# The first gather of each expert stage reads its indices from where VectorE writes them, and VectorE's first low parts wait for it

## The reference, cut to what matters

```
def ec_moe(h, w_router, w_gate, w_up, w_down):
    cap = EC_CAPACITY * length // N_EXPERTS          # 128 of 1024 tokens, 32 of 256
    aff = jax.nn.softmax((h @ w_router).astype(jnp.float32), axis=-1)
    g, idx = lax.top_k(jnp.swapaxes(aff, 1, 2), cap)
    xg = jax.vmap(lambda hb, ib: hb[ib])(h, idx)
    hid = jax.nn.silu(jnp.einsum('becd,edf->becf', xg, w_gate)) * jnp.einsum('becd,edf->becf', xg, w_up)
    out = jnp.einsum('becf,efd->becd', hid, w_down) * g.astype(h.dtype)[..., None]
    return ...                                       # each row added back at its token
```

## Time and profile before

| | us |
|---|---|
| median of 3 runs | 2653.34 |
| the runs | 2649.62 to 2656.38 |
| the profiled execution | 2649.22 |
| its span | 2647.40 |
| TensorE busy | 2354.5 (89%) |
| VectorE busy | 1793.8 (68%) |
| ScalarE busy | 1417.3 (54%) |
| GpSimd busy | 191.8 (7%) |

### The profile page before, as it was taken

How to read it: one execution, slowest core, us unless ns; L and a number is a source line. 1 busy time by engine, 2 the same in 40 slices (tenths; PEclk the granted TensorE clock), 3 DMA queues, 4 the chain that set the end, 5 groups by cost and what they waited for, 6 DMA issues and landing times.

```text
span 2647.4 us, 33888 instructions
## 1 busy us (share of the span) xinstructions
PE 2354.5 (89%) x13012; PEld 1791.6 (68%) x13012; DVE 1793.8 (68%) x1983; ACT 1417.3 (54%) x1435; POOL 191.8 (7%) x222
## 2 busy tenths in 40 slices
PE   5999998789739999999999969998791999999994
PEld 3787777568626666666666647776571788888883
DVE  5623222465577888878888756566557899999995
ACT  6400112565515666666656543666351777777773
POOL 0000000000010101101101010000000011111110
PEclk9899999899859999999999979999895999999997
DMA  6024545545306877877878751010543899999995
GB/s 241 24 84 133 164 149 132 224 168 210 141 28 262 283 289 289 296 295 285 306 274 284 295 166 29 28 44 20 200 152 135 322 394 390 388 388 388 387 379 182
DMA packets 194244, 585.53 MB, mean 221 GB/s; under 512 B 19560, under 2 KB 64352, under 8 KB 187616
## 3 DMA queue, kind: packets, MB, share of 16 engines
q1 hardware_dynamic: 178592, 529.61, 53.8%
q0 software_dynamic: 12336, 48.24, 6.7%
q10 hardware_dynamic: 3216, 6.29, 0.6%
HBM read 536.88 MB, written 47.21 MB: 221 GB/s over the span
## 4 chain that ended last, share of the span: by engine, by line
PE 84%; DVE 7%; DMA 4%; ACT 4%; issue 1%; SPq 0%; POOL 0%; ACTq 0%; POOLq 0%; DVEq 0%
PE ps L1506 14%; PE ps L1508 14%; PE ps L1507 14%; PE ps L1519 6%; PE ps L544 5%; PE ps L545 4%; PE ps L546 4%; PE ps L767 3%; PE ps L769 2%; PE ps L768 2%; PE ps L486 1%; PE ps L520 1%; PE ps L1527 1%; PE ps L581 1%; PE ps L582 1%
## 5 line engine op out<-in xcount | busy, mean ns | idle before, releaser
L1715 DVE TENSOR_TENSOR R_H_r<-R_M,R_W_r 128x2048 fp32r<-128x2048 f32 x336 | 761.3, 2288 | 148.0 <-ACT R_W_r L1620 147.9
L1620 ACT CAST R_W_r<-R_M 128x2048 fp32r<-128x2048 f32 x336 | 640.5, 1914 | 220.9 <-PE ps L1508 86.7
L1508 PE MATMUL ps<-R_W_r,R_C_r 128*128 128x512 f32 x1536 | 609.3, 397 | 0.0
L1506 PE MATMUL ps<-R_W_r,bc_r 128*128 128x512 f32 x1024 | 415.0, 405 | 13.2 <-DVE R_C_r L1733 9.5
L1507 PE MATMUL ps<-R_H_r,bc_r 128*128 128x512 f32 x1024 | 405.6, 396 | 0.0
L1508 PEld LDWEIGHTS ps<-R_W_r,R_C_r 128*128 128x128 f32 x1536 | 291.1, 190 | 66.9
L544 PE MATMUL ps<-R_H_r,R_W_r 128*128 128x512 f32 (+1 forms) x632 | 233.3, 369 | 16.6 <-DVE R_W_r L885 8.9
L1506 PEld LDWEIGHTS ps<-R_W_r,bc_r 128*128 128x128 f32 x1024 | 194.2, 190 | 70.9 <-issue 17.4
L545 PE MATMUL ps<-R_C_r,R_W_r 128*128 128x512 f32 (+1 forms) x632 | 229.3, 363 | 0.0
L546 PE MATMUL ps<-R_H_r,R_W_r 128*128 128x512 f32 (+1 forms) x632 | 228.8, 362 | 0.0
L1507 PEld LDWEIGHTS ps<-R_H_r,bc_r 128*128 128x128 f32 x1024 | 194.5, 190 | 43.2
(11 more groups left out here) (290 smaller groups left out, 3696.3 us busy)
## 6 DMA issues: line engine op xcount, KB each, us to landing
R_M<-in_moe_w_gate SPq DMA_DIRECT2D x114, 1024.0 KB, 8.2
R_M<-in_moe_w_down SPq DMA_DIRECT2D x112, 1024.0 KB, 7.7
R_M<-in_moe_w_up SPq DMA_DIRECT2D x110, 1024.0 KB, 7.4
bc<-in_ada_w SPq DMA_DIRECT2D x28, 1024.0 KB, 4.9
R_H<-in_moe_w_up SPq DMA_DIRECT2D x18, 1024.0 KB, 9.5
R_H<-in_moe_w_down SPq DMA_DIRECT2D x16, 1024.0 KB, 10.4
R_H<-in_moe_w_gate SPq DMA_DIRECT2D x14, 1024.0 KB, 10.0
R_W<-in_ev_w_in SPq DMA_DIRECT2D x25, 512.0 KB, 4.0
```

The costliest lines, as they stand in the source:

```text
L1506: pe.matmul(o, hi[:, k, :], wh[:, kk, cs], start=(k == 0), stop=False)
L1508: ins = pe.matmul(o, lo[:, k, 0:P], wh[:, kk, cs], start=False, stop=(k == KC - 1))
L1620: nc.scalar.copy(whi[j], raw[slot + j]).then_inc(unit_high_done, 1)
L1715: nc.vector.tensor_tensor(wlo[j], raw[slot + j], whi[j], ALU.subtract).then_inc(unit_low_done, 1)
```

## The change

The last of the 16 ranking rounds overwrites nothing any more, and the wait that follows it is for the index search instead. GpSimd's first gather in each layer has a function of its own, `gather_first`: it reads its indices from column 0 of `icolT` (column 32 for the context) instead of from `gidx`, with no copy, and then raises `gather_index_set` (and `context_gather_index_set`), which the copies raised before. VectorE waits for that semaphore (the context's in layer 0) before its first two low parts. GpSimd's wait for `tokens_chosen` stands behind its waits for the stores, where it stood ahead of them. The other gathers are as before.

```
             for r in range(CAPL // 8):
                 v8, i8 = tkv[0:ne, 8 * r:8 * r + 8], tki[0:ne, 8 * r:8 * r + 8]
                 own.do(nc.vector.max(v8, a))
-                nc.vector.max_index(i8, v8, a)
-                own.do(nc.vector.match_replace(a, v8, a, -2.0))
+                ins = nc.vector.max_index(i8, v8, a)
+                if r < CAPL // 8 - 1:
+                    own.do(nc.vector.match_replace(a, v8, a, -2.0))
+            own.do(ins)
...
+            dve.wait_ge(context_gather_index_set if C else gather_index_set, n0 + 1)
             low(0, 0, 0, 0, 0)
             low(0, 0, 0, 0, 1)
             token_columns(n0, 0)
...
-            def gather(count, first):
+            def gather_first():
+
+                pool.indirect_dma_start(out=xg, out_offset=None, in_=xnd,
+                                        in_offset=bass.IndirectOffsetOnAxis(ap=icolT[:, 0:1], axis=0)).then_inc(rows_gathered, 16)
+                pool.sem_inc(gather_index_set, 1)
+                if C:
+                    pool.indirect_dma_start(out=xgc[0:C, :], out_offset=None, in_=xnd,
+                                            in_offset=bass.IndirectOffsetOnAxis(ap=icolT[0:C, 32:33], axis=0)).then_inc(context_rows_gathered, 16)
+                    pool.sem_inc(context_gather_index_set, 1)
+
+            def gather(count):
...
-            pool.wait_ge(tokens_chosen, l + 1)
-
             pool.wait_ge(normed_stored, 16 * (NT if l == 0 else NT + TL))
             for b in range(2):
                 pool.wait_ge(tile_stored[b], 16 * (NT // 2 if l == 0 else NT // 2 + TL // 2))
-            gather(n0 + 1, True)
-            gather(n0 + 2, False)
+            pool.wait_ge(tokens_chosen, l + 1)
+            gather_first()
+            gather(n0 + 2)
```

More of the change, by code:

```diff
@@ L1849, in pool_moe @@
             C = CAPC if l == 0 else 0
-            def gather(count, first):
+            def gather_first():
[7 more added lines that the diff above has]
+            def gather(count):
                 n, e = count - 1, count - 1 - n0
-                if not first:
-                    pool.wait_ge(rows_gathered, n * 16)
-                    pool.wait_ge(rows_transposed, n)
+                pool.wait_ge(rows_gathered, n * 16)
+                pool.wait_ge(rows_transposed, n)
                 pool.tensor_copy(gidx[:, 0:1], icolT[:, bass.ds(e, 1)]).then_inc(gather_index_set, 1)
                 if C:
-                    if not first:
-                        pool.wait_ge(context_rows_gathered, n * 16)
+                    pool.wait_ge(context_rows_gathered, n * 16)
                     pool.tensor_copy(gidx[0:C, 1:2], icolT[0:C, bass.ds(e + 32, 1)]).then_inc(context_gather_index_set, 1)
@@ L1898, in pool_moe @@
                 pool.wait_ge(tile_stored[b], 16 * (NT // 2 if l == 0 else NT // 2 + TL // 2))
-            gather(n0 + 1, True)
-            gather(n0 + 2, False)
-            gather(n0 + 3, False)
-            gather(n0 + 4, False)
+            pool.wait_ge(tokens_chosen, l + 1)
+            gather_first()
+            gather(n0 + 2)
+            gather(n0 + 3)
+            gather(n0 + 4)
             scatter(n0 + 1, True)
             with pool.Fori(n0 + 5, n0 + NE + 1) as count:
-                gather(count, False)
+                gather(count)
                 scatter(count - 3, False)
```

## The result

| | before | after |
|---|---|---|
| median of 7 runs, us | 2650.72 | 2638.35 |
| the runs, us | 2647.34 to 2656.38 | 2635.09 to 2643.72 |
| the profiled execution, us | 2649.22 | 2639.8 |
| its span, us | 2647.4 | 2638.1 |
| mean granted clock of TensorE | 0.941 | 0.944 |

What follows compares the result with a forecast made beforehand. The prediction took TensorE to bound the kernel, with uncovered waits before each expert stage setting its start. Layer 0's 4.78 us and layer 1's 6.49 gave 11.27 off 2653.34: 2642.1 us, forecast range 2638 to 2646.

Steps and rivals of the forecast that it cites:

- the loss of 0.33 us priced for layer 0: Layer 0's context gather, blocked by a low part, lands at about +6.6, delaying the token columns; bounds 0 and 2.3 us.
- (1): Ranking in both layers: without the last MATCH_REPLACE the cast follows the index search directly; gain 0.65 us twice, 1.30.
- (2): First gathers: index copies and their wait go, VectorE releases the gather directly; gain 4.46 us in layer 0, 2.25 in layer 1.
- (3): VectorE's new wait before its low parts: they start about +0.5 us after layer 0's gather start, 0.0 in layer 1.
- tie as going to the gather: Layer 1: gather and low part start together, the gather is not blocked; landing 4.28 against 7.87 us, gain 3.59.
- (A): Rival: VectorE's low part wins layer 1's tie and blocks the gather; total gain 8.0, 2645.3 us; chance 0.24.
- Layer 1's landing: Layer 1's gathered rows land in 4.28 us instead of 7.87, gain 3.59, weight load leaving behind the gather's descriptors.
- (4): After the starts: the second gather's copy, layer 0, may inherit any of the 4.38 us that isn't VectorE's doing.
- (B): Rival: GpSimd's first use costs about 2 us on layer 0's gather; total gain 7.1, 2646.2 us; chance 0.07.
- (C): Rival: VectorE is ahead in both layers, blocking GpSimd through both low parts; only 1.30 stays, 2652.0 us; chance 0.04.
- (D): Rival: the load stream, not TensorE, sets the second expert stage; layer 1 gains nothing, 2648.6 us; chance 0.05.
- (E): Rival: TensorE's half-clock stretches lengthen by 0.74 us each, outweighing the gain; with 18, 2655.4 us; chance 0.04.

Runs made afterwards that it cites:

- e1: Changed kernel with the last MATCH_REPLACE put back; median 2637.63 us, ratio 0.9950 to the kernel before.
- e8: Changed kernel with VectorE's first two low parts waiting, in both layers, for the landing of the first gathered rows; 2639.44 us, one run.
- e4: Changed kernel with layer 1's increment ahead of the gather, so that VectorE's low part starts first; 2637.12 us, one run.
- e3: Kernel before, index copies kept, without the last MATCH_REPLACE and with VectorE's low parts waiting for the copies; 2642.29 us, ratio 0.9975.
- e6: Changed kernel without VectorE's wait, plus a small GpSimd memset in layer 0 released by the end of the ranking; 2641.64 us, one run.
- e5: As e4, with SyncE's first weight load of layer 1 held until the gathered rows have landed; 2633.32 us, one run.
- e7: Changed kernel with the wait on the gather itself, gates computed behind the token choice, token-column semaphore raised earlier; 2635.89 us, ratio 0.9949 to before.
- e9: Changed kernel without VectorE's wait in layer 1; in layer 0 it waits only for its own last token-choice operation; 2640.54 us, one run.
- e2: Changed kernel without VectorE's wait for the increment, gathers still straight; 2645.89 us, ratio 0.9980 to the kernel before.

## Where the prediction was right, and where it was wrong

The direction held, and so did the mechanism but for one step; the sizes in the sum did not all hold. The forecast was 2642.1 and the time 2638.35, 3.75 us lower, inside the range of 2638 to 2646 but only 0.35 above its lower end. The step that failed is the loss of 0.33 us priced for layer 0, which did not come. The term of the sum that was mis-sized most is its base, 2653.34 where seven runs gave 2650.72. Both are worked out below, with the terms in the prediction's order.

(1) *The last replacement.* Priced at 0.65 twice; e1 gives 0.66 and 0.61. Right. The cast starts 0.04 behind the search's end where 0.03 was said.

(2) *The copies.* The gather was to start 0.82 behind VectorE's last operation of the token choice (the copy L1309) and starts 0.85 behind it (763.68 to 764.53). From the index search to the gather it is 5.08 and 2.89 us less; 5.11 and 2.90 were priced for parts (1) and (2).

(3) *The order.* "GpSimd's queue runs ahead of its cores": right. The increment came 0.22 us before the gather, VectorE 0.56 behind it in layer 0 (0.5 said) and 0.01 ahead of it in layer 1 (0.0 said). The "tie as going to the gather" did so three times in three. That it did is the part the forecast did not earn: the starts were worked out as equal, the gather was taken as the winner with no row that says so, and 3.3 of the 11.27 us hung on it; (A) had the other outcome at 0.24. "Only the DMA's first moment is open to it" held both ways: a gather already begun loses nothing (1.01), the context's, which met a running low part, ended 0.78 behind that part's end at 767.38 (+3.6, as said).

The Trainium skill's exclusive lock ("SBUF — State Buffer", "SBUF: two separate sides") agrees with the half in which VectorE comes first, from a lead of 0.08 us on; with the lead of 0.01 in layer 1 the gather was not blocked. Its other half would hold the low part until the gather ends; a low part begun at 765.09, 0.45 us before the gather's end, was not held, nor did the two take longer (4.49 us).

**The step that failed** is the loss priced for layer 0: "ends at +2.8 + 0.8 = +3.6 [...] thus 2.9 behind its descriptors, so at about +6.6 [...] Loss 0.33". The block came as forecast, the loss did not: the columns start at +7.28, against +7.32 before. The error is in carrying the 2.9 us over from an unblocked gather. The context's rows landed 4.3 us after its start at +1.33, so at +5.6:
```profile
L1862 POOL DMA_INDIRECT R_C<-xnd,icolT x1: 2297/2297/2297, 765.9 to 765.9; - x1
DMA to landing us min/median/max: 4.3/4.3/4.3
```
That is 2.0 behind the end of its descriptors and not 2.9, so it lies 0.6 before TensorE is through with the eight transposes of the main rows (770.79). The context's transposes follow these without a gap. In e8, with the context's gather free, they end no sooner (+7.53). The lower bound, "0 (not blocked)", was the size, though not for the reason given with it. Layer 0 gained 5.11 us, and 4.78 was said: the whole of the 0.33.

*Layer 1's landing* was 4.37 us, and the transposes began 4.41 behind the gather's start; 4.28 was taken from layer 0. Hence 6.39 instead of 6.49. The reason given, descriptors not held up and the weight load not beside them, is what e4 and e5 separate: 1.59 us for the descriptors, 1.97 for the load.

*The base* is the largest piece of the miss. The forecast subtracted 11.27 from 2653.34, the median of three runs. With four more it is 2650.72, and 2649.8 and 2649.28 in 18 and 9 later ones, and a single one on another chip took 2644.66. From 2650.72 the same sum gives 2639.45. So of the 3.75 us 2.62 are the base and 0.23 the entries (11.50 instead of 11.27). The other 0.9 is no more than the runs scatter: stretches that the change does not touch differ between profiles by more, for instance from the start to the first ranking 721.78 us before, 726.84 and 723.82 in the changed kernel's two profiles, and 720.38 to 722.38 in the experiments. Which of these are the clock's doing was not separated.

(4) *What is late next.* The second gather's copy, now GpSimd's first in layer 0, takes 0.18 us (771.94 in the profile after), so nothing of the 4.38 moved there. e3 shows that there was nothing to move.

The rivals. (A) did not occur; made on purpose it costs layer 1 3.56 us, 3.3 were given. (B) falls by the changed kernel's own profile, where layer 0's gather is GpSimd's first work after 264 us and takes 1.01, and by e3 and e6. (C) named a real mechanism, low parts that keep GpSimd out through both, but put it where the wait prevents it; in layer 0 without the wait it is exactly what happens. (D) falls: with the DMA share at 1.02 as before, the way from layer 1's last index search to the end of the span went from 625.8 us to 618.2, and to 619.1 in the changed kernel's second profile. An earlier start that a load stream ate up again would have left it at 625.8. (E) falls as a one-way effect: the half-clock stretches of the two starts went from 4.01 and 5.49 us to 5.54 and 4.78.

## What to carry to other kernels

When a small GpSimd operation takes as long as a large VectorE operation beside it, order the two before you speed up the small one, and do both: here the straight gather alone gave 4.55 us and the wait with the copies kept 5.87, against 11.50 for both. Some 1.3 us in each of these is the shorter ranking, so it is 3.3 and 4.6 against 10.2. An increment behind an indirect DMA in the program is no proof that the DMA has started: read where it fires, and mind what else its waiter lets go, in e4 a weight load that cost 1.97 us. And a difference of 11 us in 2650 is found in the stretch that it touches, since the totals and the median of three runs carry 3 us of their own.

## What the runs showed of the hardware that was not expected

- Two low parts in a row blocked GpSimd as one in layer 0 whenever the first began with no idle time ahead of it (4.44 and 4.45 us, and the copy's 4.38), and left room between them with 0.20 us of idle ahead (2.53 us), and in layer 1 without any (2.29 us). The cause is open.
- Started within 0.01 us of each other, an indirect DMA and a low part cost each other next to nothing, three times in three (1.01 us for the DMA, 0.04 more for the pair of low parts). 0.08 ahead was enough for the low part to block it.
- The context's gather of layer 0 lands sooner behind the end of its descriptors when these were held up in the middle: 1.9 to 2.0 us in the seven profiles where a low part held them (the changed kernel twice, e1, e4, e5, e7, e9), against 2.6 to 2.9 in e2, e6 and e8, where it was free. The main gather did not: its transposes began 3.28 behind in e5, against 3.40 in the changed kernel. The cause is open.
- An indirect DMA that carries the wait itself starts 0.28 us behind its release, and 0.85 behind when the wait stands in the queue ahead of it with others.
